# Layer norm after the first experts moved into the second mixer, a ring of seven experts' weights, and another order for the last of them

## What the kernel computes

```
h   = LayerNorm(alpha * x + mixer(x))          # layer 0: GLA + SSD; layer 1: pooling + MoBA attention
x'  = LayerNorm(alpha * h + experts(h))        # both layers
experts: a router picks 1 of 4 groups and 2 of its 8 experts for each token;
         each of the 32 experts is silu(h @ gate) * (h @ up) @ down,
         gate and up together 1024 x 512 (2 MB), down 256 x 1024 (1 MB)
layer 1's mixer begins with  q, k, v, u = x' @ cd_w_in   (1024 x 512 each)
         and reads a paged cache of 2048 past keys and values for each of the 8 sequences
```

## Time and profile before

| | |
|---|---|
| median of 3 runs | 1254.98 us (1252.78 to 1260.91) |
| the profiled execution | 1255.12 us, of which the span of the trace is 1253.2 us |
| busy, share of the span | PE 90%, DVE 40%, ACT 18%, POOL 15% |
| mean granted clock of PE | 0.954 of full speed |
| DMA | 358.94 MB, mean 286 GB/s |
| layer 0's experts | about 357 us to 575.7 us |
| `pass_stage` | 583.7 us to 608 us |
| layer 1's mixer | 608.7 us to about 890 us |
| layer 1's experts | about 975 us to 1216.6 us, then the last stage |

### The profile page before, as it was taken

The page is one execution under the profiler, slowest core; times in us unless marked ns, Lnnn a source line. Parts: engine busy times, 40 slices in busy tenths (PEclk is TensorE's granted clock), DMA queues, the critical chain, the costliest instruction groups (busy, mean ns, idle before and its releaser), DMA issues. The chain is left out here.

```text
span 1253.2 us, 15326 instructions
## 1 busy us (share of the span) xinstructions
PE 1124.8 (90%) x5821; PEld 571.3 (46%) x5821; DVE 502.7 (40%) x1363; ACT 226.7 (18%) x511; POOL 183.0 (15%) x178
## 2 busy tenths in 40 slices
PE   8999999999999978888999899899899998888872
PEld 6874566655543323224543345545454433322230
DVE  3614765577732211113322334454986221111117
ACT  0311223321220100001411213242212110000000
POOL 0000000000011111102534552220000111110202
PEclk9999999999999989898999999999998999988995
DMA  7520200346589999995976998882936999999945
GB/s 285 192 93 1 107 33 18 126 197 283 220 331 420 419 420 420 421 420 204 383 304 233 402 338 347 325 327 99 414 144 258 368 419 419 421 421 420 406 184 213
DMA packets 84949, 358.94 MB, mean 286 GB/s; under 512 B 13940, under 2 KB 18165, under 8 KB 55174
## 3 DMA queue, kind: packets, MB, share of 16 engines
q1 hardware_dynamic: 63270, 279.67, 56.0%
q0 software_dynamic: 19520, 74.01, 15.4%
q10 hardware_dynamic: 2080, 4.19, 0.9%
HBM read 342.85 MB, written 31.16 MB: 298 GB/s over the span
## 5 line engine op out<-in xcount | busy, mean ns | idle before, releaser
L1917 PE MATMUL ahead_psum<-m_wg,top_xT 128*64 128x512 f32 x672 | 163.5, 634 | 29.4 <-DMA m_wg<-in_moe_w_gate_up 28.4
L1942 PE MATMUL n_psum_m<-m_wd,top_xT 128*64 128x512 f32 x528 | 120.6, 598 | 2.6 <-issue 2.6
L1917 PEld LDWEIGHTS ahead_psum<-m_wg,top_xT 128*64 128x64 f32 x672 | 50.8, 145 | 134.9 <-issue 96.8
L1409 PE MATMUL ahead_psum<-top_wide,top_xT 128*128 128x512 f32 x224 | 102.6, 603 | 1.5 <-PEq L158 1.5
L1917 PE MATMUL ahead_psum<-top_wide,top_xT 128*64 128x512 f32 x320 | 79.3, 642 | 22.3 <-DMA top_wide<-in_moe_w_gate_up 22.3
L1981 DVE COPY top_xT<-n_psum_t 128x512 f32<-128x512 f32 x31 | 21.4, 692 | 184.1 <-PE n_psum_t L1902 184.1
L1847 POOL DMA_INDIRECT expert_rows<-e_Y,m_dest x33 | 32.8, 994 | 378.2 <-DVE e_Y L1990 364.1
L2324 PE MATMUL ahead_psum<-top_wide,top_xT 128*128 128x512 f32 x192 | 85.2, 596 | 0.0
L2169 POOL DMA_INDIRECT cd_kv<-in_cache_kT,top_kpages x64 | 61.9, 968 | 69.0 <-PE cd_psum_d L2366 41.4
L1942 PEld LDWEIGHTS n_psum_m<-m_wd,top_xT 128*64 128x64 f32 x528 | 36.0, 136 | 62.5 <-issue 59.1
L1409 PEld LDWEIGHTS ahead_psum<-top_wide,top_xT 128*128 128x128 f32 x224 | 41.0, 192 | 44.2 <-issue 44.0
(11 more groups left out here) (502 smaller groups left out, 1682.7 us busy)
## 6 DMA issues: line engine op xcount, KB each, us to landing
m_wg<-in_moe_w_gate_up SPq DMA_DIRECT2D x88, 1024.0 KB, 26.3
m_wd<-in_moe_w_down SPq DMA_DIRECT2D x64, 1024.0 KB, 27.5
top_wide<-in_moe_w_gate_up SPq DMA_DIRECT2D x40, 1024.0 KB, 27.4
cd_kv<-in_cache_kT SPq DMA_DIRECT2D x64, 256.0 KB, 5.7
m_wg<-expert_rows SPq DMA_DIRECT2D x16, 512.0 KB, 6.4
ab_w<-in_ab_w_in SPq DMA_DIRECT2D x2, 2048.0 KB, 11.0
top_wide<-in_ab_w_in SPq DMA_DIRECT2D x2, 2048.0 KB, 7.8
top_wide<-in_ab_w_out SPq DMA_DIRECT2D x2, 2048.0 KB, 8.9
```

Source lines behind the costliest of these rows:

```text
L1409: last = nc.tensor.matmul(half_bank(i, h)[:P, :], mixT[:, k, tok0(t):tok0(t) + P], w[h][:, k, :], start=(k == 0), stop=(k == KD - 1))
L1917: last = nc.tensor.matmul(pg[i % 2][64 * a:64 * a + 64, :], xgT[i % 2][:, j, 64 * a:64 * a + 64], wg[2 * (i % NR) + a][:, j * 512:(j + 1) ...
L1942: last = nc.tensor.matmul(py[n2][64 * a:64 * a + 64, :], hT[:, j, 64 * a:64 * a + 64], wd[2 * (i % NR) + a][:, j * D + n2 * 512:j * D + (n ...
```

## The change

1. `pass_stage` is gone. Its work stands inside `mixer_cd`, interleaved with the projection of q: PE's order is 6 idle products, tile 4's transposes, 4 idle products, q's "part", tile 0's transposes, 4 idle products, the first half of q for tile 0, tile 1's transposes, the second half, and so on. DVE adds the pairs of rows for tiles 4 and 0, POOL for tiles 1 to 3, ahead of its first gathers. Q's weights are loaded at the end of layer 0's experts (`query`, after `gu` reaches 15). The rows now lie in `X` and in the second slot of the cached keys. Transposed rows are copied 4 chunks by ACT and 4 by DVE.
2. The ring is seven experts in place of three pairs. The fill takes a fifth expert ahead of the projection's end; experts 5 and 6 use `wide`. Down weights 6 lie in `X[:, 2:4]`. Loads are issued expert by expert, expert n waiting for the pair in which expert n - 7 was.
3. The last four experts' loads come in the order: gate-and-up of 28, 29, 30, 31, then down of 28, 29, 30, 31. In round 15 PE runs `gate_up(15,1)` ahead of `down(14)`. The extra pair's weights go to fixed places (in layer 1: 5 and 6), and its gathers wait for pair 14 in layer 0 and pair 13 in layer 1, and for the landing of the last gate-and-up halves as before.

```
-    RING = 3
+    RING = 7
...
+        self.wg = [M.sb(f"wg{i}", [128, KD * 2 * DE]) for i in range(self.RING - 2)] + wide
+        self.wd = [M.sb(f"wd{i}", [128, 2 * D]) for i in range(self.RING - 1)] + [X[:, 2:4, :].rearrange("p t n -> p (t n)")]
...
+    def slot(self, i, a):
+
+        if 2 * i + a < NE:
+            return (2 * i + a) % self.RING
+        return (((4, 0), (1, 2)), ((5, 6), (4, 0)))[self.l][(i - NE // 2) % 2][a]
+
+    def left(self, n):
+
+        return (n - self.RING) // 2 + 1
+
+    def load_up(self, eng, n, halves=(0, 1)):
         for h in halves:
             part = slice(2048 * h, 2048 * h + 2048)
+            row = (self.l * NE + n) * 128
+            eng.dma_start(self.wg[n % self.RING][:, part], self.w_gu[row:row + 128, part])\
+               .then_inc(self.up_in[h][n // 2 % 4], 16)
+
+    def load_down(self, eng, n):
+        row = (self.l * NE + n) * 128
+        eng.dma_start(self.wd[n % self.RING][:, :], self.w_dn[row:row + 128, :]).then_inc(self.down_in[n // 2 % 4], 16)
+
+    def reload_up(self, eng, n, half_used, multiplied):
+
+        eng.wait_ge(half_used, self.left(n))
+        self.load_up(eng, n, (0,))
+        eng.wait_ge(multiplied, self.left(n))
+        self.load_up(eng, n, (1,))
+
+    def reload_down(self, eng, n, projected):
+
+        eng.wait_ge(projected, self.left(n))
+        self.load_down(eng, n)
+
+    def fill(self, eng):
+        for i in range(2):
+            for h in range(2):
+                for a in range(2):
+                    self.load_up(eng, 2 * i + a, (h,))
             for a in range(2):
-                row = (self.l * NE + 2 * i + a) * 128
-                eng.dma_start(self.wg[2 * (i % self.RING) + a][:, part], self.w_gu[row:row + 128, part])\
-                   .then_inc(self.up_in[h][i % self.RING], 16)
-
-    def load_down(self, eng, i, experts=(0, 1)):
-        for a in experts:
-            row = (self.l * NE + 2 * i + a) * 128
-            eng.dma_start(self.wd[2 * (i % self.RING) + a][:, :], self.w_dn[row:row + 128, :])\
-               .then_inc(self.down_in[i % self.RING], 16)
-
-    def load(self, eng, i, half_used, multiplied, projected):
-
-        eng.wait_ge(half_used, i - self.RING + 1)
-        self.load_up(eng, i, (0,))
-        eng.wait_ge(multiplied, i - self.RING + 1)
-        self.load_up(eng, i, (1,))
-        eng.wait_ge(projected, i - self.RING + 1)
-        self.load_down(eng, i)
-
-    def fill(self, eng, pairs):
-        for i in pairs:
-            self.load_up(eng, i)
-            self.load_down(eng, i)
+                self.load_down(eng, 2 * i + a)
+        self.load_up(eng, 4)
+        self.load_down(eng, 4)
...
+        E.fill(sp)
         for i, (t, P) in enumerate(ORDER):
             if i == 4:
                 sp.wait_ge(summed, 10)
-                E.load_up(sp, E.RING - 1)
-                E.load_down(sp, E.RING - 1, (0,))
+                E.load_up(sp, 5)
+                E.load_up(sp, 6)
             sp.wait_ge(final, 2 * i + 2)
             sp.dma_start(rows[tok0(t):tok0(t) + P, :], X[:P, t, :]).then_inc(stored, 16)
-        E.load_down(sp, E.RING - 1, (1,))
+        E.load_down(sp, 5)
+        sp.wait_ge(stored, 16 * 5)
+        sp.wait_ge(picked, 2)
+        E.load_down(sp, 6)
...
         def weights(i):
-            pool.wait_ge(gu, i - NR + 1)
-            pool.wait_ge(dn, i - NR + 1)
+            before = (main - 2 - E.l, main - 1)[i - main] if i < main + 2 else i - 2
+            pool.wait_ge(gu, before + 1)
+            pool.wait_ge(dn, before + 1)
             if i == main:
-                pool.wait_ge(E.up_in[1][(main - 1) % NR], 32 * ((main - 1) // NR + 1))
+                pool.wait_ge(E.up_in[1][(main - 1) % 4], 32 * ((main - 1) // 4 + 1))
             for dst, src, got in ((wg, E.w_gu, wx), (wd, E.w_dn, wxd)):
                 for a in range(2):
                     at = 2 * (i - main) + a
-                    nc.gpsimd.indirect_dma_start(out=dst[2 * (i % NR) + a][:, :], out_offset=None, in_=src,
+                    nc.gpsimd.indirect_dma_start(out=dst[E.slot(i, a)][:, :], out_offset=None, in_=src,
                                                  in_offset=bass.IndirectOffsetOnAxis(ap=E.widx[:, at:at + 1], axis=0))\
-                        .then_inc(got[i % NR], 16)
+                        .then_inc(got[i % 2], 16)
...
+        E.reload_up(sp, 7, gh, gu)
+        E.reload_down(sp, 7, dn)
+        for n in range(8, NE - 4, 2):
+            E.reload_up(sp, n, gh, gu)
+            E.reload_up(sp, n + 1, gh, gu)
+            E.reload_down(sp, n, dn)
+            E.reload_down(sp, n + 1, dn)
+        for n in range(NE - 4, NE):
+            E.reload_up(sp, n, gh, gu)
+        for n in range(NE - 4, NE):
+            E.reload_down(sp, n, dn)
+        if lines:
+            sp.dma_start(X[0:1, 4, :], lines[0].partition_broadcast(1)).then_inc(line_in, 16)
+            sp.dma_start(xT[0:1, 4:8, 256:512], lines[1].rearrange("(o k n) -> o k n", o=1, k=4)).then_inc(line_in, 16)
+        if query:
+            sp.wait_ge(gu, main - 1)
+            sp.dma_start(query[0], query[1]).then_inc(query[2], 16)
         sp.wait_ge(all_landed, 1)
-        load_rows(sp, combine_rows(E), yd, y_in, ORDER[:2])
+        load_rows(sp, y, yd, y_in, ORDER[:2])
...
-                if i > behind:
+                if i > behind and i != main - 1:
                     down(i - 1)
                 if i < hi:
                     gate_up(i, 1)
+                if i == main - 1:
+                    down(i - 1)
...
+            sp.dma_start(gbT[:, :, :], A["ln2_T"]).then_inc(gb_in, 16)
+            load_rows(sp, y, y_dram, y_in, ORDER[2:])
+            sp.dma_start(w[1][:, :, :], pieces[:, :, 1024:1536]).then_inc(w_in[1], 16)
             sp.dma_start(newS[:, :, :].rearrange("p g n -> p (g n)"), A["pool_state_T"]).then_inc(small_in, 16)
             sp.dma_start(pscale[:, :], A["pool_scale_T"]).then_inc(small_in, 16)
             sp.dma_start(wp[:, :, :], A["cd_w_pool"].rearrange("g c d -> c g d")).then_inc(small_in, 16)
-            sp.wait_ge(w_in[0], 16)
             loads.k_plain(sp, 0)
+            for i, (t, P) in enumerate(ORDER):
+                sp.wait_ge(normed, i + 1)
+                sp.dma_start(kept[tok0(t):tok0(t) + P, :], X[:P, t, :]).then_inc(rows_stored if i else sample_stored, 16)
             loads.k_plain(sp, 1)
...
-            pool.wait_ge(w_in[0], 16)
+            pool.wait_ge(first_paired, 2)
+            for t, P in ORDER[2:]:
+                pool.wait_ge(y_in[t], 32)
+                nc.gpsimd.tensor_tensor(y[t][:P, 0, :], y[t][:P, 0, :], y[t][:P, 1, :], ALU.add).then_inc(paired, 1)
             for n in range(8):
+                if n == 1:
+                    pool.wait_ge(normed, 5)
...
+            front, back = range(KD // 2), range(KD // 2, KD)
+            idle_products(nc, C, bc, 6)
+            normal(0)
+            idle_products(nc, C, bc, 4)
             project("q", "part")
-            project("q", 0)
+            normal(1)
+            idle_products(nc, C, bc, 4)
+            project("q", 0, front)
+            normal(2)
+            project("q", 0, back)
             project("q", 4)
-            project("q", 1)
+            project("q", 1, front)
+            normal(3)
+            project("q", 1, back)
+            project("q", 2, front)
+            normal(4)
+            project("q", 2, back)
             turn("q", 4)
             turn("q", 0)
-            project("q", 2)
+            project("q", 3)
             turn("q", 1)
             score(0)
-            project("q", 3)
+
+            project("k", "part")
...
+            normal(0)
+            normal_copies(0)
+            normal(1)
             evict("q", "part")
+            normal_copies(1)
+            normal(2)
+            normal(3)
+            normal_copies(2)
             evict("q", 0)
             evict("q", 4)
+            normal(4)
+            normal_copies(3)
             evict("q", 1)
+            normal_copies(4)
+            evict("q", 2)
             copy_turned("q", 4)
             copy_turned("q", 0)
-            evict("q", 2)
-            copy_turned("q", 1)
             evict("q", 3)
             load(3, 0)
+            copy_turned("q", 1)
...
+            normal(0)
+            normal(1)
+            normal_copies(0)
+            normal(2)
+            normal_copies(1)
+            normal(3)
+            normal(4)
+            normal_copies(2)
+            normal_copies(3)
+            dve.wait_ge(sample_stored, 16)
             c.add(V.memset(Q[:, :, :, :], 0.0))
             for u in uP:
                 c.add(V.memset(u[:, 0:PBUF], 0.0))
-            c.wait()
-            def p_both(i):
-                p_maxima(i)
-                p_norm(i)
-
             rotate("q", 4)
             rotate("q", 0)
+            normal_copies(4)
             rotate("q", 1)
+            c.wait()
             build_q()
             rotate("q", 2)
+            dve.wait_ge(rows_stored, 16 * 4)
...
```

(1 more changed line is left out.)

242 lines of the change are left out of this document (112 added, 130 removed).

## The result

The changed kernel takes 1244.01 us (median of 20 runs, 1238.47 to 1251.92) against 1256.70 us beside it (20 runs). The ratio is 0.9902, 95% interval 0.9884 to 0.9921: faster by 1.0%, where the forecast was 1256 us and no change. The profiled execution took 1240.65 us, with a span of 1238.7 us, 14.5 us less than the one before. Two executions further down, of the kernel before and of a_mixer_clean, are slow ones (1298.8 and 1349.5 us, at a mean granted clock of 0.896 and 0.828), and they are left out of every comparison.

The account below looks back on a forecast made before the run. Weight traffic was taken to bound layer 0's expert stages except at both ends, and PE the mixer. Terms -2.8 - 0.9 + 0.5 + 4 = +0.8 us on 1255.1 us gave 1256 us, range 1242 to 1266.

Parts of the forecast that it names:

- Layer 1's tail: End of layer 1's experts: the extra pair's gathers slow the last four downs, shifting the extra pair by +4 us.
- downs undisturbed: Rival for layer 1's tail: plain loads keep their pace beside the gathers, layer 1 gains 7 us: 1245 us, chance 0.14.
- Downs that come early in spite of the gathers: Layer 1's tail: down weights coming early beside the extra pair's gathers would show the prediction wrong; no size given.
- The ring: Expert weight loads, both layers: of a fifth expert's 7.5 us lead, one load, 2.5 us, remains.
- the hole at 350 to 365 us: Layer 0, SP's loads of experts 7 and 8: a hole in the DMA windows, forecast at 350 to 362.
- The end of the weights: Both layers' experts: the end of the weights comes 2.5 us earlier, bounds 0 and 7.5.
- Layer 0's tail: End of layer 0's experts: waits and an issue gap of PE go, -2.8 us, bounds -5 and 0.
- The combining stage: Merged into the mixer: q begins earlier, but waits and transposes fall among projections; -0.9 us, bounds -6 and +3.
- The scratch: Smaller descriptor store for POOL's key gathers in the mixer: some may wait, +0.5 us, bounds 0 and +13.
- the rival of 1269 us: Mixer: key gathers each cost POOL 2.288 us, making steps 4 to 7 late, together about 13 us; chance 0.09.
- The likeliest case: Whole kernel: the forecast's own case, 1250 to 1262 us, chance 0.40.
- the chance of "same": Whole kernel: time within about 1% of the kernel before, chance 0.75; faster 0.15, slower 0.10.

Follow-up runs that it names:

- a_mixer_clean: Kernel before with only the combining stage moved inside the mixer; old ring, orders of loads and default scratch kept: 0.9985 of the kernel before.
- after_third: The changed kernel measured once more, unaltered, beside another kernel on the same chip: 0.9950 of the kernel before.
- a_ring6: Changed kernel with a ring of six experts in place of seven; last order, mixer and scratch as changed: 0.9981 of the kernel before.
- b_scratch: Kernel before with the 2 KB scratch for descriptors alone: 0.9971 of the kernel before.
- a_mixer_clean2: Repeat of the kernel before with only the combining stage moved inside the mixer: 0.9965 of the kernel before.
- a_early: Changed kernel with the extra pair's rows and weights gathered ahead of pair 13's scatter, without the wait for up_in: layer 1 went from 227.5 to 237.5 us.

## Why the prediction was wrong

**The failed step is "Layer 1's tail"** (+4 us, bounds -7 and +9). The sharing that it describes is real, price included: beside gathers the downs get a third, `down(15)` waits 7.65 to 8.95 us and then runs at the low clock (5.93 to 6.37 us for 16 instructions), and layer 1 takes 235.2 us in after_third, inside the forecast's 232.6 to 239.1 (its 1195.5 to 1202 against 962.86). What failed is the time at which the gathers' data flow, put at 2 us behind their issue with 5.0 us of downs left (2.1 MB at 420 GB/s), because before the change nothing stood ahead of them. There it is indeed 1.7 us. In the changed kernel pair 13's scatter and the extra pair's rows stood there, 1.3 us ahead of one another, and the data came 5.1 to 6.4 us behind the issue. In two of three profiles the scatter also held the issue itself back, and only about half a load of downs was left (0.53 and 0.45 MB): then the tail gives 6 us in place of costing 4, as in the rival "downs undisturbed" (0.14), though for another reason than the one given there. In the third 0.97 MB were left, and that was enough to starve `down(15)`. Downs that come early in spite of the gathers are also what the prediction named as a sign of being wrong. I had the order of POOL's instructions before me and looked only at the last wait.

**The ring** was sized about right: one load of lead, the hole at 350 to 365 us as described, 2.6 to 3.6 us per layer by a_ring6's stages. The end of the weights, forecast 2.5 us earlier, came 1.6 us earlier in layer 0 (its last plain packet starts 221.6 us behind the first `gate_up` in the mean of six profiles, against 223.3 before) and 4.2 to 4.4 in layer 1 where the downs escaped (220.6 to 220.8 against 225.0).

**Layer 0's tail** has the right size: -2.8 forecast, 3.2 us measured in the tail, 2.7 in the whole layer (228.4 in the mean of the six profiles with this code, against 231.1 in before, b_scratch and a_mixer_clean2). Part of that is luck: the order of halves costs the steady stretch about 2 us, which the forecast left out, and the ring gives the layer somewhat more than its 2.5.

**The combining stage** had its mechanism and places right and its size low: -0.9 forecast, -3.8 measured. This is the second term that failed, by its size. Tile 4's transposes came at 591.97 (591.4 forecast), "part" at 595.49 (595), q for tile 0 at 601.93 behind 1.77 us (603, 1.9), q for tile 1 behind 2.54 us (2.9). So q began 1.1 us earlier than forecast, and from its first product to k's first full projection it took 41.8 us and not 43.5. The listed terms add up to 43.3, and the timeline has most of them a little shorter: q 27.8 from start to start in place of 28.4, transposes 2.6 (3.2), the small product with the wait 3.6 (3.9), score(0) and k's part 5.3 (5.5). The forecast laid the old durations end to end, while in the trace one instruction starts 0.1 to 0.2 us before the one ahead of it ends. Together these are 2.8 us at that point, nearly all of the miss.

**The scratch** was +0.5 and is 0 or a small gain (1.2 us in the final stage); the rival of 1269 us (0.09) didn't come.

**Sum.** With -3.8 for the mixer, -2.7 for layer 0 and -7.4 for layer 1 and what follows (282.9 and 283.1 against 290.4) it is -13.9, 1241; with a starved down the last is +0.2 and it is 1249. The changed kernel's runs cover both, and the first mixer's length spreads either by several us more. How many of its runs starve isn't known, as only three were profiled. The range held the median of 1244, but not by the forecast's reasons: it lies between two ways of going, of which the forecast had only the longer, with the mixer's gain too small in both. The likeliest case and the chance of "same" did not come.

## What to carry to other kernels

A gather's data start when what stands ahead of it in the software queue has moved, not when it is issued: 1.7 us behind the issue with nothing there, 5.1 to 6.4 us behind a scatter and a gather of rows. Before pricing two streams that meet, write down what stands ahead of each in its own queue. Where a program has a close race between a prefetch and the loads that are read next, give the prefetch an explicit wait on the load that should win (here pair 14's downs), and take that of several which leaves about one load open: one further held too long and one less starved PE. And judge a change in parts before keeping it whole: here the order of halves took back some 2 us per layer (layer 1 takes 225.0 to 226.6 without it and 227.5 to 227.7 with it, where nothing starves).

## What the runs showed of the hardware

The software and the hardware queue, when both had work, shared the DMA engines by turns of one packet, whichever had the larger ones: 229 packets against 226 in 12 us (a_early), of 15.2 KB against 7.3, and 113 against 116 in 3 us (after_third, 1171 to 1174 us), of 4.0 KB against 7.2. So the queue with the larger packets gets the more bytes. In a_early the plain loads fell from 420 to 137 GB/s (1.64 MB in 12 us), by which a load of 1.05 MB takes 7.7 us in place of 2.5, an estimate from these two rates.

A wait can pay. PE's low clock behind a wait of 5.3 us (6.29 us for a half, against 3.65) delayed a scatter by 2 us, and layer 1 ended 7.6 us earlier than in after_third. That the one made the other is read from the order of events in four profiles; no run changed the clock alone.

With PE busy throughout, the granted clock in the first mixer differed between executions of the same code: 1.00, 0.96 and 0.69 in the stretch from 140 to 160 us. The execution at 0.69 has a first mixer of 352.6 us, 6 to 9 us above most others (343.5 to 346.9). a_ring6 has 352.4 us at 0.95 there, so that stretch isn't the only cause; no run here shows why.
